# Grid attention with the values as weights in both column halves, and the sinks' exponentials for eight steps at once

## The chip, the cores and the metric

One core of one Trainium2 chip runs the whole program. The metric is the device time in microseconds, the median of the runs. All times below are microseconds.

## The reference

A block of two transformer layers is followed by a second block of two. The second block's first mixer, called the grid mixer here, is the part that is changed: grouped-query attention with 16 query heads over 4 groups of keys and values, head width 64, over 256 context tokens and 256 latent tokens, with a learned sink in the softmax.

```python
def softmax_with_sink(s, sink):
    sk = sink.astype(jnp.float32)[None, :, :, None, None]
    m = jnp.maximum(jnp.max(s, axis=-1, keepdims=True), sk)
    e = jnp.exp(s - m)
    return e / (jnp.sum(e, axis=-1, keepdims=True) + jnp.exp(sk - m))

# context tokens attend to the 256 context keys
s_c = jnp.einsum('bqhgd,bkhd->bhgqk', q_ctx, k_ctx)
o_ctx = jnp.einsum('bhgqk,bkhd->bqhgd', softmax_with_sink(s_c, sink_g), v_ctx)
# latent tokens attend to latent keys at most 128 away and to all context keys
p = softmax_with_sink(jnp.concatenate([s_lat, s_ctx], axis=-1), sink_g)
o_lat = einsum(p[..., :n_loc], v) + einsum(p[..., n_loc:], v_ctx)
return o_lat @ w_o, o_ctx @ w_o
```

## The kernel before, in words

Each engine has its own program, written out in order, and the engines meet through counting semaphores (`up` raises one, `wait_ge` waits for a named point of it). An engine runs its list strictly in order, so an instruction that waits holds everything behind it. Large products are made of three passes of fp32r (high times high, high times low, low times high); the attention itself is in plain fp32, where TensorE makes two passes of each matmul. A weight chunk comes by DMA into `raw`, ScalarE (ACT) rounds it into `WH` (line 439), VectorE (DVE) makes the rest `WL` (line 452), two chunks ahead of use (`act_begin`, `dve_begin`).

The grid mixer (`grid_pe`, `grid_act`, `grid_dve`, `grid_pool`) first projects keys, values and the queries of group 0. Then comes a loop of 34 **slots**. Slot n = 8g + p works on pair p of group g. A pair is two heads on the same 128 query tokens; the two heads' queries stand in the two halves of the partitions. Pairs 0 to 3 of a group (`seg` 0) are the context tokens with 256 keys (n=256), pairs 4 to 7 the latent tokens with 512 keys (n=512). In the text a slot is named by its p. In slot n TensorE does, in this order:

1. `scores` of pair n into PSUM banks 4 and 5, which must have been read by DVE;
2. one step of `queries(g+1)`, while g < 3: in p0 to p3 a quarter of the projection of the next group's queries (24 passes), in p7 eight transposes of those queries, nothing in p4 to p6;
3. `pv` (probabilities times values) of pair n-2 and `turn_p` (transposes of the probabilities) of pair n-1, each head by head: pv even, turn even, pv odd, turn odd.

In `pv` the turned probabilities `cPT` (128 keys x 128 queries) are the weights and 64 columns of the values are moved, so the output has the queries on the partitions: 2 matmuls a head for n=256, 4 for n=512, each two passes. All 8 steps of a `seg` go into bank 7.

DVE adds the mask and takes the maximum (line 2455), copies the sink behind the scores (2456), and makes the negated maximum (2458), once for each head; then it copies the odd head's turned probabilities (2467). ACT takes the exponential with its sum (2401), so the sink is the 257th or 513th element; it copies the even head's turned probabilities (2410) between the two exponentials, and evacuates the projected queries in p4 (2383, 2385) and their transposes in p7 (2393). After 8 steps DVE takes the reciprocal of the sums (2474) and multiplies bank 7 into `cO` (2478), which frees the bank. In p0 of groups 1 and 2, ACT rounds a weight chunk behind its two exponentials, and DVE makes the low part ahead of the odd head's copy.

After slot 33 `turn_o_pe` turns the whole output (32 transposes) and ACT and DVE split it into `XH` and `XL` (1113, 1120); then the output products (`last_products_pe`) begin. They go through features 0 to 511 of all four output blocks before they come to feature 512, and two of the weight chunks are made long before.

Of the kernel before, what the change touches and what calls it, by code (L numbers as in the profile page):

```python
# [8 lines left out]
F32 = mybir.dt.float32  # L9
# [6 lines left out]
KT = 8  # L16
# [133 lines left out]
class Program:  # L150
# [106 lines left out]
    def phase_views(self):  # L257
# [30 lines left out]
        self.cSM = [v(H, 5120 + 520 * i, [128, 520]) for i in range(2)]  # L288
        self.cSM += [v(H, 11280, [128, 520]), v(self.tmp_at, 3072, [128, 520])]
        self.cPT = [v(H, 6160 + 512 * i, [128, 512]) for i in range(2)]  # L290
        self.cO = v(H, 7184, [128, 4096]).rearrange("p (b d) -> p b d", b=4)
# [823 lines left out]
    def turn_o_dve(self, tag, h):  # L1115
        dve = self.dve
        for k2 in range(4):
# [3 lines left out]
            self.xl.name((tag, 2 * k2 + 1))  # L1121

# [1104 lines left out]
    def grid_pe(self):  # L2227
# [87 lines left out]
        def pv(g, i):  # L2315
            seg, hd, o = self.GRID_STEPS[i]
            n = 4 if seg else 2
            pe.wait_ge(self.emptied if i % 2 else self.evac, ("grid", "p", g, i))
# [5 lines left out]
            m.then_inc(*self.weighed.up(("grid", g, i)))  # L2324
            if i % 8 == 7:
                self.empties([7], (self.o_done, ("grid", g, seg)))
# [4 lines left out]
        for n in range(34):  # L2331
# [6 lines left out]
            for j in range(2):  # L2338
                if n > 1:
                    g, p = divmod(n - 2, 8)  # L2340
                    pv(g, 2 * p + j)
                if 1 <= n < 33:
                    g, p = divmod(n - 1, 8)
                    turn_p(g, 2 * p + j)
        for h in range(2):
            self.turn_o_pe(f"go{h}", self.cO[:, 2 * h:2 * h + 2, :], (self.o_done, ("grid", 3, 1)), h)
        self.rest_grid = self.last_products_pe("grid", w_o, self.x_both(("go0", "go1")), None, True)

    def grid_act(self):
# [4 lines left out]
        nm, dens = self.small[:, 108:112], [self.small[:, 160 + 8 * i:168 + 8 * i] for i in range(2)]  # L2354
# [40 lines left out]
        def score(g, i):  # L2395
            seg, hd, o = self.GRID_STEPS[i]
            u, n = i % 4, 512 if seg else 256
            act.wait_ge(self.v_step, ("grid", "neg", g, i))
            if g:
                act.wait_ge(self.v_step, ("grid", "recip", g - 1, seg))  # L2400
            act.e.activation(self.cSM[u][:, 0:n + 1], self.cSM[u][:, 0:n + 1], ACT.Exp, bias=nm[:, u:u + 1], scale=0.125, accum_out=dens[seg][:, 4 * o + hd:4 * o + hd + 1]).then_inc(*self.expd.up(("grid", g, i)))
# [9 lines left out]

        for _ in queries(0):
# [14 lines left out]
        for h in range(2):  # L2427
            self.turn_o_act(f"go{h}", h)
        self.last_products_act("grid", True, 0, 0, [(self.turned, ("go1", "o", 3))])

    def grid_dve(self):
        dve, PS = self.dve, self.PS
        sk8 = self.small[:, 88:104]
        mx, nm = self.small[:, 104:108], self.small[:, 108:112]
# [10 lines left out]
        def score(g, i):  # L2445
            seg, hd, o = self.GRID_STEPS[i]
            b, u, n = 4 + i % 2, i % 4, 512 if seg else 256
            SM = self.cSM[u]
            col = sk8[:, 4 * g + hd:4 * g + hd + 1]
            dve.wait_ge(self.scored, ("grid", g, i))  # L2450
            dve.wait_ge(self.ld_masks, "grid")
            dve.wait_ge(self.v_step, ("grid", "sink"))
            if (g, i) > (0, 3):
                dve.wait_ge(self.turned, ("grid", "p", g, i - 4) if i > 3 else ("grid", "p", g - 1, i + 12))
# [14 lines left out]
        def pv(g, i):  # L2469
            if i % 8 < 7:  # L2470
                return
# [552 lines left out]
```

## Time and profile before

| | us |
|---|---|
| median of 3 runs (lowest, highest) | 2503.65 (2498.86, 2504.4) |
| the profiled execution: its own time | 2499.47 |
| the profiled execution: its span | 2498.2 |
| busy in the span: TensorE matmuls | 2326.4 (93%) |
| busy: VectorE | 1221.8 (49%) |
| busy: ScalarE | 969.2 (39%) |
| busy: GpSimd | 506.6 (20%) |
| mean granted TensorE clock | 0.961 |
| grid mixer's loop, first scores to last `pv` | from 1437.2 to 1580.2 |
| first output product | 1586.91 |

Busy time is a share of the whole span, over stages with different limits. The granted clock is a share of 2.4 GHz; its two levels are 1 and 0.5. In the tables of instructions PE is TensorE's matmuls and PEld its weight loads, and both carry the line of a helper: 466 for matmuls, 475 for transposes.

### The profile page before, as it was taken

The numbers are of one execution on the slowest core, as the hardware profiler recorded it, in microseconds if no ns is written. First come the engines' busy times: TensorE is split into PE (matmuls) and PEld (weight loads), VectorE is DVE, ScalarE is ACT, GpSimd is POOL, SyncE is SP. The second block draws the span as 40 slices with busy tenths as digits, with TensorE's granted clock in tenths as the row PEclk, the third lists the DMA queues.
The fourth block names the chain that finished last, engine by engine and source line by source line (L and its number), as shares of the span: only waits on it lengthen the run. The fifth ranks groups of instructions, "written<-read, shape, count | busy, mean of one in ns | idle before, by whom it ended". The sixth has DMA issues, their size and how long they took to land.

```text
span 2498.2 us, 37765 instructions
## 1 busy us (share of the span) xinstructions
PE 2326.4 (93%) x16663; PEld 2120.0 (85%) x16663; DVE 1221.8 (49%) x1521; ACT 969.2 (39%) x1145; POOL 506.6 (20%) x453
## 2 busy tenths in 40 slices
PE   6999999989999999889999899979999989888998
PEld 6998899979999998557999877867888877657997
DVE  5645566646555543445655345362122264545444
ACT  3433344434343433334444244333222233534442
POOL 2112434302111211220221101012202210230220
PEclk9999999989999999789999999989999999999999
DMA  6555433445555555666554310113332322213551
GB/s 242 175 173 173 139 122 133 136 169 174 182 179 185 180 182 173 229 237 236 172 183 155 124 35 18 34 68 101 101 98 88 102 96 85 68 51 93 181 183 68
DMA packets 205245, 344.72 MB, mean 138 GB/s; under 512 B 8845, under 2 KB 69498, under 8 KB 205082
## 3 DMA queue, kind: packets, MB, share of 16 engines
q1 hardware_dynamic: 205082, 342.31, 41.0%
q8 instruction: 131, 2.15, 0.3%
q14 instruction: 32, 0.26, 0.0%
HBM read 341.24 MB, written 1.05 MB: 137 GB/s over the span
## 4 chain that ended last, share of the span: by engine, by line
PE 80%; DVE 9%; POOL 4%; ACT 4%; issue 2%; SPq 0%; DMA 0%; DVEq 0%; POOLq 0%; ACTq 0%
PE PS L466 77%; PE PS L475 3%; DVE WL L452 2%; ACT WH L439 1%; POOL small L1454 1%; DVE rstd L587 1%; DVE XL L634 1%; POOL TMP L1463 1%; DVE XL L1002 0%; DVE al L998 0%; POOL small L1452 0%; DVE TMP L1382 0%; POOL TMP L1464 0%; DVE TMP L1387 0%; DVE al L1371 0%
## 5 line engine op out<-in xcount | busy, mean ns | idle before, releaser
L452 DVE TENSOR_TENSOR WL<-raw,WH 128x2048 fp32r<-128x2048 f32 (+2 forms) x281 | 651.6, 2331 | 720.7 <-ACT WH L439 720.7
L466 PE MATMUL PS<-XH,WH 128*128 128x256 f32 (+1 forms) x2336 | 699.3, 299 | 40.3 <-issue 15.3
L466 PE MATMUL PS<-XL,WH 128*128 128x256 f32 (+1 forms) x2336 | 692.9, 297 | 0.0
L466 PE MATMUL PS<-XH,WL 128*128 128x256 f32 (+1 forms) x2336 | 692.6, 297 | 0.0
L439 ACT ACTIVATE WH<-raw 128x2048 fp32r<-128x2048 f32 (+2 forms) x281 | 518.8, 1858 | 361.6 <-PE PS L466 361.1
L466 PEld LDWEIGHTS PS<-XH,WH 128*128 128x128 f32 x2336 | 451.6, 193 | 56.6 <-issue 18.5
L466 PEld LDWEIGHTS PS<-XL,WH 128*128 128x128 f32 x2336 | 452.6, 194 | 10.1
L466 PEld LDWEIGHTS PS<-XH,WL 128*128 128x128 f32 x2336 | 452.2, 194 | 10.0
L466 PE MATMUL PS<-WH,XH 128*128 128x256 f32 (+2 forms) x944 | 287.3, 304 | 17.3 <-DVE XL L634 8.5
L466 PE MATMUL PS<-WL,XH 128*128 128x256 f32 (+2 forms) x944 | 279.1, 296 | 0.0
L466 PE MATMUL PS<-WH,XL 128*128 128x256 f32 (+2 forms) x944 | 278.9, 295 | 0.0
L466 PE MATMUL PS<-HH,WH 128*128 128x256 f32 x960 | 273.5, 285 | 3.4 <-DVE WL L452 3.4
L466 PE MATMUL PS<-HL,WH 128*128 128x256 f32 x960 | 272.9, 284 | 0.0
L466 PE MATMUL PS<-HH,WL 128*128 128x256 f32 x960 | 272.8, 284 | 0.0
L466 PE MATMUL PS<-al,al 128*128 128x64 f32 (+8 forms) x1376 | 224.5, 342 | 16.5 <-DVE al L2882 6.0
L466 PEld LDWEIGHTS PS<-al,al 128*128 128x128 f32 (+4 forms) x1376 | 164.3, 196 | 64.5 <-issue 37.1
L466 PEld LDWEIGHTS PS<-WH,XH 128*128 128x128 f32 x944 | 186.0, 197 | 35.3 <-issue 22.2
L466 PEld LDWEIGHTS PS<-HH,WH 128*128 128x128 f32 x960 | 185.6, 193 | 3.6 <-DVE WL L452 3.6
L466 PEld LDWEIGHTS PS<-WL,XH 128*128 128x128 f32 x944 | 186.4, 197 | 2.5
L466 PEld LDWEIGHTS PS<-WH,XL 128*128 128x128 f32 x944 | 186.2, 197 | 2.5
L466 PEld LDWEIGHTS PS<-HL,WH 128*128 128x128 f32 x960 | 185.6, 193 | 0.1
L466 PEld LDWEIGHTS PS<-HH,WL 128*128 128x128 f32 x960 | 185.5, 193 | 0.0
(232 smaller groups left out, 2573.2 us busy)
## 6 DMA issues: line engine op xcount, KB each, us to landing
raw<-in_ffn_w_in SPq DMA_DIRECT2D x88, 1024.0 KB, 5.1
raw<-in_w_mod SPq DMA_DIRECT2D x48, 1024.0 KB, 5.2
raw<-in_ffn_w_out SPq DMA_DIRECT2D x40, 1024.0 KB, 4.9
raw<-in_a_w_in SPq DMA_DIRECT2D x36, 1024.0 KB, 4.9
raw<-in_w_mlp_in SPq DMA_DIRECT2D x32, 1024.0 KB, 5.5
raw<-in_w_mlp_out SPq DMA_DIRECT2D x32, 1024.0 KB, 5.0
raw<-in_gla_w_in SPq DMA_DIRECT2D x12, 1024.0 KB, 5.0
raw<-in_attn_w_qkv SPq DMA_DIRECT2D x6, 1024.0 KB, 5.0
```

Source lines behind the costliest of these rows:

```text
L439: act.e.activation(self.WH[q % NW][:, 0:nk * nn], self.raw[j % NRAW][:, 0:nk * nn], ACT.Copy).then_inc(*self.hi.up(j))
L452: dve.e.tensor_tensor(self.WL[j % NRAW][:, 0:nk * nn], self.raw[j % NRAW][:, 0:nk * nn], wh.bitcast(F32), ALU.subtract).then_inc(*self.lo. ...
L466: return self.pe.e.matmul(out, l, r, start=start, stop=stop, skip_group_check=skip)
L475: return self.pe.e.transpose(out, i, self.ident if n == 128 else self.CST[0:n, IDENT:IDENT + n])
L587: dve.e.reciprocal(rs, rs).then_inc(*self.rstd_.up(tag))
L634: dve.e.scalar_tensor_tensor(self.XL[slot][:, k, :], R[:, k, :], self.COL[:, at + k:at + k + 1], self.XH[slot][:, k, :].bitcast(F32), ALU. ...
L1454: pool.e.tensor_tensor(rs, rs, self.MH[:, 0:8], ALU.pow).then_inc(*self.p_step.up(key("pow")))
L1463: pool.e.tensor_tensor(q[:, :, :, 0:32], x[:, :, :, 32:64], bc(0, 32), ALU.mult)
```

## The change

In `pv` the operands change places. 64 columns of the values are the weights, and the turned probabilities of 128 queries are moved. The even head's output goes to partitions 0 to 63, the odd head's to 64 to 127, that is to the two column halves of the array, with the two heads' matmuls alternating. The output has its features on the partitions, as the output products need it. So the 32 transposes at the end go away, and the division can no longer be by a number per partition. The reciprocals, one per query and head, are spread by ACT to 64 columns each (`cRD`, 128x512) and turned by TensorE (`sums`, 4 transposes per group and `seg`), ACT copies bank 7 to `cO`, DVE multiplies `cO` by the turned reciprocals, and ACT and DVE split the result into `XH` and `XL`, partly in slots 27 to 33. The two heads' `pv` stand together, ahead of both `turn_p`. The sink is no longer a column of the scores: one negation serves two heads, and per 8 steps DVE makes an argument of 8 columns, ACT its exponential, and DVE adds it to the sums.

```diff
+        def pv(g, i0):
+            seg, hd, o = self.GRID_STEPS[i0]
+            pair, n = hd // 2, 4 if seg else 2
+            pe.wait_ge(self.evac, ("grid", "p", g, i0))
+            pe.wait_ge(self.emptied, ("grid", "p", g, i0 + 1))
             pe.wait_ge(self.evac, ("grid", "in", 5, 1))
-            if i % 8 == 0:
+            if i0 % 8 == 0:
                 self.pe_bank(7)
             for k in range(n):
-                m = self.mm(PS[:, 7, o * 256 + hd * 64:o * 256 + hd * 64 + 64], self.cPT[i % 2][:, k * 128:k * 128 + 128], self.cV[:, k, g * 64:g * 64 + 64], k == 0, k == n - 1)
+                for j in range(2):
+                    m = self.mm(PS[64 * j:64 * j + 64, 7, pair * 256 + o * 128:pair * 256 + o * 128 + 128], self.cV[:, k, g * 64:g * 64 + 64], self.cPT[j][:, k * 128:k * 128 + 128], k == 0, k == n - 1, True)
...
+            if i0 % 8 == 6:
+                self.empties([7], (self.evac, ("grid", "o", g, seg)))
+                sums(g, seg)
+        def sums(g, seg):
+            nonlocal spare
+            b = spare = self.GRID_SPARE[spare]
+            pe.wait_ge(self.evac, ("grid", "r", g, seg))
+            self.pe_bank(b)
+            for pair in range(2):
+                for o in range(2):
+                    m = self.tr(PS[:, b, pair * 256 + o * 128:pair * 256 + o * 128 + 128], self.cRD[:, 256 * o + 128 * pair:256 * o + 128 * pair + 128])
...
-            for j in range(2):
-                if n > 1:
-                    g, p = divmod(n - 2, 8)
-                    pv(g, 2 * p + j)
-                if 1 <= n < 33:
-                    g, p = divmod(n - 1, 8)
+            if n > 1:
+                g, p = divmod(n - 2, 8)
+                pv(g, 2 * p)
+            if 1 <= n < 33:
+                g, p = divmod(n - 1, 8)
+                for j in range(2):
                     turn_p(g, 2 * p + j)
-        for h in range(2):
-            self.turn_o_pe(f"go{h}", self.cO[:, 2 * h:2 * h + 2, :], (self.o_done, ("grid", 3, 1)), h)
```

On ACT:

```diff
+            if i % 8 == 7:
+                act.wait_ge(self.v_step, ("grid", "sinks", g, seg))
+                act.e.activation(e8, e8, ACT.Exp).then_inc(*self.expd.up(("grid", "sinks", g, seg)))
+        def recips(g, seg):
+            act.wait_ge(self.v_step, ("grid", "recip", g, seg))
+            if g or seg:
+                act.wait_ge(self.turned, ("grid", "r", g, 0) if seg else ("grid", "r", g - 1, 1))
+            act.e.activation(self.cRD.rearrange("p (h d) -> p h d", d=64), rd.unsqueeze(2).to_broadcast([128, 8, 64]), ACT.Copy).then_inc(*self.evac.up(("grid", "r", g, seg)))
+        def out(g, seg):
+            act.wait_ge(self.weighed, ("grid", g, 8 * seg + 7))
+            act.e.activation(self.cO[:, seg, 2 * g:2 * g + 2, :], PS[:, 7, :].rearrange("p (k t) -> p k t", k=2), ACT.Copy).then_inc(*self.evac.up(("grid", "o", g, seg)))
         for n in range(34):
             g, p = divmod(n, 8)
+            if n > 4 and n % 4 == 1:
+                recips(*divmod(n // 4 - 1, 2))
...
+            if n > 4 and n % 4 == 1:
+                out(*divmod(n // 4 - 1, 2))
+            if 27 <= n < 33:
+                seg, g3 = divmod(n - 27, 3)
+                split(g3, seg)
+            if n == 33:
+                split(3, 0)
+        split(3, 1)
...
```

On DVE:

```diff
+        def score(g, i0):
+            for i in (i0, i0 + 1):
...
+                dve.e.tensor_tensor_reduce(self.cSM[u][:, 0:n], PS[:, b, 0:n], self.CST[:, 512 * o:512 * o + n], 1.0, sk8[:, 4 * g + hd:4 * g + hd + 1], ALU.add, ALU.max, mx[seg][:, c:c + 1]).then_inc(*self.maxed.up(("grid", g, i)))
+            dve.wait_ge(self.maxed, ("grid", g, i0 + 1))
+            dve.e.tensor_scalar(nm[seg][:, c - 1:c + 1], mx[seg][:, c - 1:c + 1], -0.125, None, ALU.mult).then_inc(*self.v_step.up(("grid", "neg", g, i0)))
...
+        def out(g, seg):
+            O = self.cO[:, seg, 2 * g:2 * g + 2, :]
+            dve.wait_ge(self.evac, ("grid", "o", g, seg))
+            dve.wait_ge(self.turned, ("grid", "r", g, seg))
+            dve.e.tensor_tensor(O, O, PS[:, self.bank_of["grid", "r", g, seg], :].rearrange("p (k t) -> p k t", k=2), ALU.mult).then_inc(*self.o_done.up(("grid", g, seg)))
         for n in range(34):
             g, p = divmod(n, 8)
+            if n and n % 4 == 0:
+                recips(*divmod(n // 4 - 1, 2))
+            if n > 4 and n % 4 == 2:
+                out(*divmod((n - 2) // 4 - 1, 2))
             if n < 32:
                 score(g, 2 * p)
-                score(g, 2 * p + 1)
```

On DVE, `recips(g, seg)` waits for the exponential of the sinks, adds it to the sums and takes the reciprocal; it stands ahead of the scores of p4 and p0. On ACT the spreading stands ahead of the exponentials of p5 and p1, and the copy of bank 7 behind them.

## Rows read from the trace of the kernel before

**Rows 1.** The page: chain that ended last, share of the span by engine.

```profile
PE 80%; DVE 9%; POOL 4%; ACT 4%; issue 2%; SPq 0%; DMA 0%; DVEq 0%; POOLq 0%; ACTq 0%
```

**Rows 2.** Busy time by stretch: start:end length, engines busy (instructions), granted clock, DMA.

```profile
1508.00:1546.00 38.00, 35.80 (x277) 29.80 (x277) 19.80 (x79) 17.47 (x45) 4.62 (x8) 1.00 0.09 29
...
1581.20:1584.60 3.40, 3.36 (x16) 3.36 (x17) 1.39 (x2) 1.69 (x3) 0.00 (x0) 0.50 0.00 0
```

**Rows 3.** Groups by form, 1438 to 1582: busy, mean ns of one | idle before.

```profile
L466 PE MATMUL PS<-al,al 128*128 128x64 f32 x384 | 51.7, 271 | 3.7 <-DVE al L2478 3.7
...
L2455 DVE CUSTOM_DVE_ANT_0 al<-PS,CST,small 128x512 f32<-128x512 f32 x32 | 23.8, 745 | 6.9 <-PE PS L466 6.9
```

**Rows 4.** Timeline of weight loads in the later GLA mixer: start, length, what.

```profile
2169.66 0.64 PEld L466 LDWEIGHTS PS<-al,al 128*64 128x64 f32 x8 [0.33 <-issue]
2170.68 0.73 PEld L466 LDWEIGHTS PS<-al,al 128*128 128x128 f32 x4 [0.39 <-issue]
2171.74 0.64 PEld L466 LDWEIGHTS PS<-al,al 128*64 128x64 f32 x8 [0.33 <-issue]
```

**Rows 5.** Timeline of weight loads, p4 to p7 of group 1 (64*128: scores).

```profile
1495.13 0.30 PEld L466 LDWEIGHTS PS<-al,al 64*128 64x128 f32 x4 [0.17 <-issue]
1496.19 0.52 PEld L466 LDWEIGHTS PS<-al,al 128*128 128x128 f32 x4 [0.76 <-issue]
...
1498.02 0.33 PEld L466 LDWEIGHTS PS<-al,al 64*128 64x128 f32 x4 [0.57 <-DVE small L2455]
...
1500.98 0.30 PEld L466 LDWEIGHTS PS<-al,al 64*128 64x128 f32 x4 [0.17 <-DVE small L2455]
...
1505.56 0.30 PEld L466 LDWEIGHTS PS<-al,al 64*128 64x128 f32 x4 [0.17 <-issue]
...
1510.93 0.42 PEld L475 LDWEIGHTS PS<-CST,al 128*128 128x128 f32 x4 [1.23 <-ACT al L2401]
1511.52 0.30 PEld L466 LDWEIGHTS PS<-al,al 64*128 64x128 f32 x4 [0.17 <-issue]
```

**Rows 6.** Timeline of DVE and ACT in the same p4.

```profile
1496.30 0.75 DVE L2455 CUSTOM_DVE_ANT_0 al<-PS,CST,small 128x512 f32<-128x512 f32 x1 [0.63 <-PE PS L466]
...
1497.28 0.72 ACT L2401 ACTIVATE al<-al,small 128x513 f32<-128x513 f32 x1 [1.78 <-DVE small L2458]
...
1498.00 0.36 ACT L2410 ACTIVATE al<-PS 128x256 f32<-128x256 f32 x1
1498.26 0.71 ACT L2401 ACTIVATE al<-al,small 128x513 f32<-128x513 f32 x1
...
1498.97 0.58 ACT L2383 ACTIVATE TMP<-PS 128x512 f32<-128x512 f32 x1
1499.44 0.59 ACT L2385 ACTIVATE TMP<-PS 128x512 f32<-128x512 f32 x1
```

**Rows 7.** Timeline of all engines, p0 (from 1473.1) and p1 (from 1479.3) of group 1.

```profile
1478.13 0.60 ACT L2410 ACTIVATE al<-PS 128x512 f32<-128x512 f32 x1 [3.02 <-PE PS L475]
...
1479.12 1.90 ACT L439 ACTIVATE WH<-raw 128x2048 fp32r<-128x2048 f32 x1
...
1481.05 2.29 DVE L452 TENSOR_TENSOR WL<-raw,WH 128x2048 fp32r<-128x2048 f32 x1 [6.00 <-ACT WH L439]
...
1483.26 0.68 DVE L2467 COPY al<-PS 128x512 f32<-128x512 f32 x1
```

**Rows 8.** Chain that ended last, 1430 to 1620: start, length, what.

```profile
1503.90 0.44 PE PS L475 x4
1504.35 0.84 PE PS L466 x8
...
1578.27 1.90 PE PS L466 x16
...
1580.19 0.22 DVE small L2474
...
1586.91 33.20 PE PS L466 x186
```

More of the change, by code:

```diff
@@ L1121, in turn_o_dve, with split_o_act, split_o_dve @@
             self.xl.name((tag, 2 * k2 + 1))
+    def split_o_act(self, tag, g, h, O, ready):
+        for signal, key in ready:
+            self.act.wait_ge(signal, key)
+        self.act.e.activation(self.XH[h][:, 2 * g:2 * g + 2, :], O, ACT.Copy).then_inc(*self.xh.up((tag, 2 * g)))
+    def split_o_dve(self, tag, g, h, O):
+        self.dve.wait_ge(self.xh, (tag, 2 * g))
+        self.dve.e.tensor_tensor(self.XL[h][:, 2 * g:2 * g + 2, :], O, self.XH[h][:, 2 * g:2 * g + 2, :].bitcast(F32), ALU.subtract).then_inc(*self.xl.up((tag, 2 * g)))
+        self.xl.name((tag, 2 * g + 1))
     def attn_out_pe(self, tag, O, ready, w_out):
@@ L2353, in grid_act @@
         KD = TMP[:, 1024:3072].rearrange("p (b g u d) -> p b g u d", b=4, g=4, u=2)
-        nm, dens = self.small[:, 108:112], [self.small[:, 160 + 8 * i:168 + 8 * i] for i in range(2)]
+        nm, dens = [self.small[:, 32 + 8 * i:40 + 8 * i] for i in range(2)], [self.small[:, 160 + 8 * i:168 + 8 * i] for i in range(2)]
+        e8, rd = self.small[:, 48:56], self.small[:, 116:124]
         self.act_begin()
@@ L2426, in grid_act @@
                 next(nxt, None)
-        for h in range(2):
-            self.turn_o_act(f"go{h}", h)
-        self.last_products_act("grid", True, 0, 0, [(self.turned, ("go1", "o", 3))])
+            if n > 4 and n % 4 == 1:
[6 more added lines that the diff above has]
+        split(3, 1)
+        self.last_products_act("grid", True, 0, 0, [(self.xl, ("go1", 6)), (self.weighed, ("grid", 3, 15))])
     def grid_dve(self):
@@ L2433, in grid_dve @@
         sk8 = self.small[:, 88:104]
-        mx, nm = self.small[:, 104:108], self.small[:, 108:112]
+        mx, nm = [[self.small[:, at + 8 * i:at + 8 * i + 8] for i in range(2)] for at in (16, 32)]
+        e8 = self.small[:, 48:56]
         dens, rd = [self.small[:, 160 + 8 * i:168 + 8 * i] for i in range(2)], self.small[:, 116:124]
@@ L2492, in grid_dve @@
                 turn_p(g, 2 * p + 1)
-            if n > 1:
-                g, p = divmod(n - 2, 8)
-                pv(g, 2 * p + 1)
-        for h in range(2):
-            self.turn_o_dve(f"go{h}", h)
+            if 28 <= n < 34:
+                seg, g3 = divmod(n - 28, 3)
+                split(g3, seg)
+        out(3, 1)
+        split(3, 0)
+        split(3, 1)
         self.last_products_dve("grid", True, 0, 0, None)
@@ L2534, in gla_sp @@
         wd = self.gWD.rearrange("p (k e r) -> p k e r", e=2, k=KT)
-        sp.wait_ge(self.o_done, ("grid", 3, 1))
+        sp.wait_ge(self.xl, ("go1", 6))
         sp.e.dma_start(self.CST[:, 0:512], A["const"][:, RESET:RESET + 512]).then_inc(*self.ld_masks.up("reset"))
```

71 lines of the change are left out of this document (33 added, 38 removed).

## The prediction

> **What bounds the kernel now.** I read four views. First the page's chain of work that ended last: TensorE carries 80% of it, DVE and ACT 13% together [rows 1]. So a change pays if it takes time from TensorE's own queue, or from a wait of that queue. Second, busy time by stretch: in the loop of slots TensorE is busy 35.8 of 38 us at the full clock [rows 2], so the loop is nearly, but not quite, TensorE's. Third, the groups by form: the old `pv` is 384 passes of 64 columns [rows 3]. Fourth, timelines and the chain, for the waits. p4 takes 2.9 us, p5 3.0, p6 4.6, p7 6.0 [rows 5], 16.4 together, and in each TensorE waits somewhere: in p7 its transposes wait 1.23 for ACT. The whole end, from the last `pv` at 1580.2 to the first output product at 1586.9, is a hand-over in which TensorE only turns [rows 8]. I write S for the start of a slot's scores.
>
> **What TensorE does less.** Eight old passes (one head, n=512) take 0.84 [rows 8], a pair 1.68; with n=256 half of it, 0.84. There are 16 pairs of each: 40.3 us. The trace of before has no probabilities moved past 64-wide weights, but the GLA mixer has plain fp32 passes into column halves: eight of 256 columns take 1.02 (2169.66 to 2170.68), no more than four full-width ones (2170.68 to 2171.74, 1.06) [rows 4]. So the halves run side by side. A new pair with n=512 is 16 passes of 128 columns, the same columns: 1.02. With n=256 it is half, 0.51, plus about 0.1, as the drain at the ends doesn't shrink: 0.6. Bounds: 0.9 and 1.9 for the large pair (the latter if they ran one after another), 0.5 and 1.0 for the small. New total 16 x 1.62 = 25.9, a gain of 14.4. Against it: going over to column halves costs 0.1 where a projection stands before it (12 pairs, 1.2; four transposes of 0.44 plus the switch to the scores are 0.59 in [rows 5]), and `sums` adds 4 transposes, 0.44 [rows 8], seven times in the loop: 3.1. TensorE's own work falls by 10 us.
>
> The Trainium skill (TensorEngine Tiling (Array Packing), Theoretical Speedup) gives up to 2x for a dimension of 64; rows 4 agree, 1.02 against 1.06 for twice the passes. The same page (PSUM Bottleneck) says that tiling doesn't speed up the emptying of PSUM; by the first rule alone the loop would gain the 10 us, by the second nothing, and the walk below shows which holds.
>
> **What the waits do.** I walk the queues with the durations of the rows. On ACT an exponential of 512 takes 0.72, a copy of 256 0.26 and of 512 0.48 until the next may start, the two evacuations 1.06 [rows 6]. DVE's first maximum starts 1.17 after S, and before it is followed by exponential 1 after 0.98 [rows 5, 6]; now both maxima (2 x 0.745 [rows 3]) and one negation come first, so exponential 1 starts 1.7 after the first maximum. New small operations are taken as 0.2, from the reciprocal's 0.22 [rows 8]; the spread copy as 0.6, from 0.59 [rows 6] (bounds 0.2 and 0.8); DVE's multiplication as 0.7, from the copy's 0.68 [rows 7]. `pv` now wants both heads' copies at once, and between the odd turn and that `pv` stand only scores.
>
> *p4.* DVE's first maximum waits 0.3 for the sinks' exponential and the sum. The next scores wait for the maxima: 2.9, as before.
>
> *p5.* Exponential 1 of p4 starts 3.05 after p4's S. ACT's queue then holds 0.72, copy 0.26, 0.72, evacuations 1.06, spread copy 0.6: 3.4. So the spread reciprocals are there at 6.5, that is 3.55 after p5's S. `sums` waits for them from 1.9 on (1.65 us idle), then 0.44, two turns 0.88, switch 0.1: p5 lasts 5.0 instead of 3.0. Behind `sums` the turns wait, and for them ACT and DVE.
>
> *p6.* Bank 7 is free after ACT's exponential, copy, exponential and copy of the bank, 6.5 after p5's S, 1.5 after p6's; before, it waited for DVE's division. 1.5 + 1.02 + 0.88, with the next scores waiting for maxima behind the multiplication: 3.7 instead of 4.6.
>
> *p7.* Exponential 1 at 2.9, 0.72, copy 0.5 (its turn ends about 3.4), 0.72, the sinks 0.2, evacuation 0.6: the second turn's bank is free 5.7 after S, then 0.44 and 0.1: 6.3 instead of 6.0. It idles 2.2 us, as TensorE arrives earlier and ACT later.
>
> Sum of p4 to p7: 17.9 against 16.4. The same walk over the old queues gives 16.2, so its latencies are 0.1 to 0.2 short: +1.6.
>
> *p0 and p1* (groups 1, 2). The old odd copy ends at 1483.94, at the end of a chain: turn, ACT's copy at 1478.13, `WH` at 1479.12, `WL` at 1481.05, copy at 1483.26 [rows 7], 10.9 after p0's S. The chain is bound to the turn, which now comes 0.2 to 0.3 later in p0 (1.02 and a switch instead of 0.84), so nothing on TensorE can shorten it. Before, the even `pv` and a turn ran under it; now the whole pair waits 2.0 us, then 1.02, `sums` 0.44, turns 0.46, switch 0.1. From 11.2: 13.2 against 12.2 (1473.1 to 1485.3): +1.0.
>
> *p2, p3:* 0.6 + 0.1 instead of 0.84: -0.1 each. *Group 3* has no projections: its first four slots gain 0.5, the rest loses 0.9, its last `pv` 0.1 earlier: +0.3. *Group 0* has nothing in flight in p0: p2 to p7 alone, +1.4.
>
> Loop: 2 x (1.6 + 1.0 - 0.2) + 1.4 + 0.3 = +6.5. The 10 us of TensorE's work come back as waits, and more: ACT's queue sets p5 and p7, the weight chunk p1.
>
> **The end.** From 1580.2 (`pv`'s result seen by DVE) to 1586.9 there are 6.7 us, 6.9 from TensorE's last pass [rows 8]. Now `sums` takes 0.44 and the products follow at once: weights of two chunks are made, features 0 to 255 split. The last output (copy, multiplication, two splits, 3 us) is wanted only at feature 768, after more than 10 us of products. -6.4. ACT's and DVE's eight splits are moved, not added: seven lie in slots with a free projection step or at the end. SP's waiting DMA of GLA's constants is hidden by the MLP that follows.
>
> Sum at full clock: +6.5 - 6.4 = +0.1. The walk came out short on the old queues, never long, so I take +0.5.
>
> **The clock.** Before, the loop ran at 1.00, and the only fall was after TensorE idled in the end part: 3.4 us at 0.50 [rows 2], inside the 6.9 already counted. New are ten idles of 1.6 to 2.3 us (p5 four times, p7 three, p1 two, one in group 3), longer than that before the fall (about 1.1). A fall of 3.4 us at half rate costs up to 1.7. I take two falls: +2.5 to 3.4. The Trainium skill (TensorE: Matmul & The Clock Gate, What's actually happening) has the clock fall after an idle window and rise after a busy one; the fall at 1581.2 agrees, and it says nothing of how partial idles in this loop count.
>
> Forecast: +0.5 + 2.5 = +3. The sum is made in one profiled execution of 2498.2 span and 2499.47 own time, 4.2 under the median of the runs, 2503.65; a difference carries over: **2506.7**. Its own range is 2501 to 2511.
>
> **Rivals.**
> *The waits don't grow (faster).* If ACT's queue in p5 and p7 is shorter than walked (spread copy 0.2, exponentials back to back), only the end counts and perhaps part of the 10 us: -6 to -16, 2488 to 2498. For: 35.8 of 38 us busy [rows 2]. Against: old waits are there already, and each new one has its queue in the rows. It decides if the loop's growth stays under 1.4, that is under 0.35 a group. Chance 0.15.
> *The clock falls at most of the ten idles.* 6 to 10 falls of 1.7: +10 to +17, 2514 to 2521. For: shorter idles have done it. Against: the old waits of p6 and p7 (0.8, 1.2) never did. Chance 0.25.
> *The halves run one after another.* 16 x (0.85 + 0.4) less what waits swallow: +16, 2520. Against: rows 4. Chance 0.04.
> *Forecast:* 0.56.
>
> **Chances and range.** What a measurement of this kernel can tell from no change is about 0.2%, 5 us: 2498.6 to 2508.7. Faster 0.15, from the first rival. Same 0.45, four fifths of the forecast's case. Slower 0.40: the two other rivals, 0.29, and the forecast's upper fifth, 0.11. The range that leaves out most of the first rival and the top of the others is 2498 to 2518.
>
> **What would show it.** In the profile after: 64-wide loads with eight starts in about 0.9 us (else the third rival); in p5 four transposes that wait some 1.6 us for ACT's spread copy, in p7 a turn that waits 2.2 for ACT's evacuation, in p1 a `pv` that waits 2.0 for DVE's copy behind `WL`; p4 to p7 near 18 us; the loop 6 to 8 us longer at full clock and the first product within 1 us of the last `pv`; stretches at 0.50 between 1437 and 1590 counted. The prediction is wrong if the loop is not longer, or if the clock falls often.

## The result: 0.17% slower, and the profile after

| | before | changed |
|---|---|---|
| median, us (runs) | 2498.86 (20) | 2504.94 (20) |
| lowest to highest | 2495.84 to 2504.52 | 2502.82 to 2506.79 |
| profiled execution: own time, span | 2499.47, 2498.2 | 2504.21, 2502.9 |
| first scores to first output product | 1437.19 to 1586.91, 149.7 | 1437.62 to 1590.76, 153.1 |
| granted clock, mean | 0.961 | 0.958 |

The ratio is 1.0017, 95% interval [1.0011, 1.0023]: slower by 0.17%, about 4 us. That is a real difference, and it lies within the 0.2% that the prediction named as "the same". The 2503.65 of the small table above was the median of three runs that lay high. Against the 20 runs the medians are 6.1 apart, against the ratio 4.2.

The chain that ended last has the shape of [rows 1], with TensorE's share a little lower:

```profile
PE 78%; DVE 9%; ACT 5%; POOL 4%; issue 3%; SPq 0%; DMA 0%; DVEq 0%; POOLq 0%; ACTq 0%
```

In the code of the changed kernel TensorE's helper lines stand one further: 467 for matmuls, 476 for transposes. Busy time by stretch (columns as in [rows 2]) shows what happened to TensorE in the loop:

```profile
1470.00:1508.00 38.00, 32.00 (x244) 24.70 (x240) 14.47 (x45) 17.07 (x44) 2.37 (x5) 0.91 0.09 29
1508.00:1546.00 38.00, 33.16 (x268) 25.30 (x264) 17.09 (x52) 16.10 (x44) 2.24 (x4) 0.96 0.09 29
...
1517.80:1521.20 3.40, 3.40 (x17) 2.75 (x15) 1.78 (x8) 0.60 (x2) 0.00 (x0) 0.52 0.02 5
```

It was busy 35.8 of 38 us in [rows 2] at the full clock. Now it is busy 33.2 and 32.0, the granted clock is 0.96 and 0.91, and inside these stretches stand pieces of 3.4 us at half clock. DVE is less busy too (17.1 against 19.8). No engine became fuller; all of them wait more.

The two profiles don't start the loop alike, and [rows 2] doesn't show that: in the kernel before the clock is at half until 4.0 us after the first scores, in the changed kernel until 1.6 after them.

```profile
1437.19:1441.20 4.01, 4.01 (x18) 3.36 (x18) 1.27 (x8) 3.88 (x7) 0.00 (x0) 0.50 0.00 0
```

```profile
1437.60:1439.20 1.60, 1.60 (x7) 0.93 (x7) 0.32 (x1) 1.45 (x2) 0.00 (x0) 0.51 0.00 0
```

Group 0's p0, the same work in both, takes 5.47 in the first and 4.39 in the second. The 1.1 us between them are in every comparison of these two loops, and they don't come from the change: a second profile of the kernel before (below) has 4.39 there with the same code. Of the profiles below, five begin like the changed kernel: the low part behind the copy, the spread copy twice, the kernel before with two orders, the first of the sinks' kernel and the second of the kernel before. All others begin like the first profile of before.

The groups by form, first scores to first product:

```profile
L476 PE MATMUL PS<-CST,al 128*128 128x128 f32 x220 | 32.6, 287 | 11.9 <-ACT al L2423 6.2 <-ACT al L2448 5.7
...
L467 PE MATMUL PS<-al,al 128*64 128x128 f32 x381 | 28.3, 283 | 9.5 <-DVE al L2524 5.7 <-ACT al L2455 2.6 <-ACT al L2442 0.6
```

The new `pv` is 28.3 us of busy time where the old one was 51.7 [rows 3]. Behind the bar stand the new idles: 11.9 us ahead of transposes, for ACT's evacuation of the turned queries (2423) and for ACT's spread reciprocals (2448), and 9.5 ahead of `pv`, mostly for DVE's copy (2524).

The weight loads of p4 to p7 of group 1, to be laid beside [rows 5]. Scores are the `64*128` rows and start the slots; `128*64` is the new `pv`:

```profile
1499.81 0.30 PEld L467 LDWEIGHTS PS<-al,al 64*128 64x128 f32 x4 [0.17 <-issue]
1500.86 0.42 PEld L467 LDWEIGHTS PS<-al,al 128*64 128x64 f32 x8 [0.76 <-ACT al L2442]
1501.45 0.42 PEld L476 LDWEIGHTS PS<-CST,al 128*128 128x128 f32 x4 [0.17 <-issue]
1502.51 0.33 PEld L467 LDWEIGHTS PS<-al,al 64*128 64x128 f32 x4 [0.64 <-DVE small L2508]
1503.77 0.42 PEld L467 LDWEIGHTS PS<-al,al 128*64 128x64 f32 x8 [0.93 <-ACT al L2442]
1505.96 1.29 PEld L476 LDWEIGHTS PS<-CST,al 128*128 128x128 f32 x12 [1.77 <-ACT al L2448]
1507.42 0.30 PEld L467 LDWEIGHTS PS<-al,al 64*128 64x128 f32 x4 [0.17 <-issue]
1508.99 0.88 PEld L467 LDWEIGHTS PS<-al,al 128*64 128x64 f32 x16 [1.27 <-ACT al L2455]
1510.04 0.86 PEld L476 LDWEIGHTS PS<-CST,al 128*128 128x128 f32 x8 [0.17 <-issue]
1511.07 0.32 PEld L467 LDWEIGHTS PS<-al,al 64*128 64x128 f32 x4 [0.17 <-DVE small L2508]
...
1516.88 0.42 PEld L476 LDWEIGHTS PS<-CST,al 128*128 128x128 f32 x4 [2.27 <-ACT small L2433]
1517.47 0.34 PEld L467 LDWEIGHTS PS<-al,al 64*128 64x128 f32 x4 [0.17 <-issue]
```

A large pair takes 1.05 (1508.99 to 1510.04), a small one 0.59 (1500.86 to 1501.45). p5 starts at 1502.51; its twelve transposes (four of `sums`, eight turns) are held for 1.77 by the spread copy and p5 lasts 4.9. p7 starts at 1511.07 and its second turn is held for 2.27. Here the label names ACT's small exponential (2433), but that one had been done for 0.6 us; what is missing is the evacuation right behind it on ACT (2423), as the same wait on the matmul side says (2.06 there).

ACT in the same p4 and p5, to be laid beside [rows 6]:

```profile
1502.64 0.72 ACT L2430 ACTIVATE al<-al,small 128x512 f32<-128x512 f32 x1 [1.97 <-DVE small L2510]
...
1503.36 0.36 ACT L2442 ACTIVATE al<-PS 128x256 f32<-128x256 f32 x1
1503.62 0.71 ACT L2430 ACTIVATE al<-al,small 128x512 f32<-128x512 f32 x1
...
1504.33 0.58 ACT L2413 ACTIVATE TMP<-PS 128x512 f32<-128x512 f32 x1
1504.80 0.59 ACT L2415 ACTIVATE TMP<-PS 128x512 f32<-128x512 f32 x1
1505.28 0.63 ACT L2448 ACTIVATE al<-small 128x512 f32<-128x512 f32 x1
```

From 1502.64 to 1505.9 ACT has not a gap, and the spread copy stands last. It reads only eight numbers per partition, and the reciprocal that makes them had ended at 1501.1, 4.2 us before.

p1 of group 1 (its scores start at 1480.8), to be laid beside [rows 7]:

```profile
1481.49 1.90 ACT L440 ACTIVATE WH<-raw 128x2048 fp32r<-128x2048 f32 x1
...
1483.43 2.29 DVE L453 TENSOR_TENSOR WL<-raw,WH 128x2048 fp32r<-128x2048 f32 x1 [7.27 <-ACT WH L440]
1485.63 0.68 DVE L2524 COPY al<-PS 128x512 f32<-128x512 f32 x1
...
1486.46 1.54 PE L467 MATMUL PS<-al,al 128*64 128x128 f32 x16 [1.87 <-DVE al L2524]
```

TensorE had turned the odd head's probabilities by 1480.9. They lay in PSUM for 4.7 us, until DVE's copy at 1485.63: 2.5 us of that are the last part of DVE's idle of 7.27, for its next instruction was `WL`, which waited for ACT, and 2.2 are `WL` itself. The pair then took 1.48 (1486.46 to 1487.94) instead of 1.03, as the clock fell 0.5 us after it had begun.

And the end, the chain that ended last:

```profile
1589.32 1.09 PE PS L467 x16
1591.00 29.04 PE PS L467 x155
```

The last `pv` ends at 1590.4. Behind it stand only the four transposes of `sums`, and the first product's matmul begins at 1590.76, 0.4 us later (this chain counts it from the end of the transposes, 1591.00). In the kernel before the same distance was 6.7, from 1580.2.

### The profile page after: what moved, and what is told of

It is laid out like the page before. It is cut to its first block, busy times and chain, and to the rows that moved or that the text cites. A ratio compares the mean times of both kernels' runs of the same rounds, so it can differ in the third digit from the quotient of the medians.

```text
span 2502.9 us, 37728 instructions
## 1 busy us (share of the span) xinstructions
PE 2315.0 (92%) x16663; PEld 2102.0 (84%) x16663; DVE 1216.8 (49%) x1433; ACT 976.9 (39%) x1169; POOL 506.7 (20%) x453
## 3 DMA queue, kind: packets, MB, share of 16 engines
HBM read 341.24 MB, written 1.05 MB: 137 GB/s over the span
## 4 chain that ended last, share of the span: by engine, by line
PE 78%; DVE 9%; ACT 5%; POOL 4%; issue 3%; SPq 0%; DMA 0%; DVEq 0%; POOLq 0%; ACTq 0%
PE PS L467 75%; PE PS L476 3%; DVE WL L453 2%; ACT WH L440 1%; POOL small L1467 1%; DVE rstd L588 1%; DVE XL L635 1%; POOL TMP L1476 1%; ACT al L2430 0%; DVE XL L1003 0%; DVE al L999 0%; POOL small L1465 0%; ACT al L2442 0%; DVE TMP L1395 0%; POOL TMP L1477 0%
## 5 line engine op out<-in xcount | busy, mean ns | idle before, releaser
L467 PE MATMUL PS<-al,al 128*128 128x64 f32 (+9 forms) x1376 | 199.9, 344 | 23.0 <-DVE al L2948 6.1
L467 PEld LDWEIGHTS PS<-al,al 128*128 128x128 f32 (+4 forms) x1376 | 135.6, 180 | 74.0 <-issue 30.6
```

The source lines that it names most:

```text
L467: return self.pe.e.matmul(out, l, r, start=start, stop=stop, skip_group_check=skip)
```

## The experiments

All times below are medians. "Mixer" is first scores to first output product in the profile of that kernel. It compares code better than a span, for this reason: from the first product on, all kernels here run the same code, and yet that part took 909.3 to 917.6 us from profile to profile, with 70 to 91 us of it at half clock. The clock makes differences inside the mixer too: 1.1 us by its start, as said above, and 1.1 to 1.6 for each fall. The order of the list is that of the argument; each of the first four undoes one order that the change had brought or left in place.

**Negation for each head.** In `score` on DVE the negation goes back into the loop over the two heads.

```diff
-            dve.wait_ge(self.maxed, ("grid", g, i0 + 1))
-            dve.e.tensor_scalar(nm[seg][:, c - 1:c + 1], mx[seg][:, c - 1:c + 1], -0.125, ...)
+                dve.wait_ge(self.maxed, ("grid", g, i))
+                dve.e.tensor_scalar(nm[seg][:, c:c + 1], mx[seg][:, c:c + 1], -0.125, ...)
```

> The changed kernel, but DVE negates each head's maximum right behind it, as before the change, instead of one negation for both. Theory of the queues: ACT's first exponential of a pair starts 0.7 us earlier, which shortens p5's wait for the spread copy by 0.8 in each of four groups, but DVE's second maximum ends 0.13 later in the slots that wait for it; together 2 to 3 us faster than the changed kernel. Rival, the clock: the ten new waits matter only through falls of the clock; the long waits of p7 and p1 stay, so nothing changes (within 1 us).

Measured: 2502.98 (11 runs), ratio to before 1.0016 [1.0005, 1.0027]; mixer 151.6, against 153.1 of the changed kernel. p4 to p7 17.2 instead of 17.7: p5 4.01 (4.88), p6 3.85 (3.66), p7 6.38 as before. Exponential 1 starts earlier, so p5's spread copy does; in p7 it changes nothing, as ACT waits there for the turn, not for the negation. It gives about 2 us, as the theory of the queues had it (1.6 by the mixers, 2.6 when the slower start of this profile is taken off).

**The turned reciprocals one slot later.** On TensorE `sums` moves from behind `pv` of the last pair to behind the turns of the slot.

```diff
-                sums(g, seg)
...
                 for j in range(2):
                     turn_p(g, 2 * p + j)
+            if n > 4 and n % 4 == 1:
+                sums(*divmod(n // 4 - 1, 2))
```

> The changed kernel, but TensorE turns the spread reciprocals behind the turns of the probabilities of the same slot instead of ahead of them. Theory of the queues: p5's wait of 1.65 us becomes one of 0.8, four times, and part of it comes back at bank 7 in p6: 2 to 3 us faster than the changed kernel. Rival: what the turns are spared, the multiplication by the turned reciprocals loses; no change within 1 us.

Measured: 2500.39 (11), 1.0008 [0.9999, 1.0017]; mixer 151.3. p5 4.00, p6 3.95, p4 to p7 17.1. The wait itself fell from 1.77 to 0.75:

```profile
1502.39 0.85 PEld L476 LDWEIGHTS PS<-CST,al 128*128 128x128 f32 x8 [0.17 <-issue]
1504.00 0.42 PEld L476 LDWEIGHTS PS<-CST,al 128*128 128x128 f32 x4 [0.75 <-ACT al L2449]
...
1506.43 0.88 PEld L467 LDWEIGHTS PS<-al,al 128*64 128x64 f32 x16 [1.55 <-ACT al L2456]
```

A part comes back in p6, where `pv` waits 1.55 for the copy of bank 7 (1.27 in the changed kernel): ACT is the same distance behind, TensorE only arrives earlier. The mixer is 1.8 shorter, 2.9 with the start taken off: the theory's 2 to 3.

**The low part of the weight chunk behind the odd head's copy.** On DVE, `WL` and the copy change places in p0.

```diff
-                if g < 3 and p == 0:
-                    self.dve_begin()
             if 1 <= n < 33:
                 g, p = divmod(n - 1, 8)
                 turn_p(g, 2 * p + 1)
+            if n < 24 and n % 8 == 0:
+                self.dve_begin()
```

> The changed kernel, but in p0 DVE makes the low part of the weight chunk behind the odd head's copy instead of ahead of it. Theory of the queues: the 2.0 us wait of the value products in p1 goes, twice, less what the later low part costs (nothing, it is made two chunks ahead), and one of the three falls of the clock with it: 3.5 to 5 us faster than the changed kernel. Rival: the wait is TensorE's arrival and moves to the next slot's maxima or to the low part's user, then 0 to 1 us.

Measured: 2500.35 (11), 1.0004 [0.9995, 1.0012]; mixer 149.4, 3.8 less (forecast 3.5 to 5). p1 5.84 in both groups, where it was 9.00 (with a fall of the clock) and 7.68. DVE in the same place:

```profile
1480.05 0.69 DVE L2524 COPY al<-PS 128x512 f32<-128x512 f32 x1 [4.78 <-PE PS L476]
1482.54 2.29 DVE L453 TENSOR_TENSOR WL<-raw,WH 128x2048 fp32r<-128x2048 f32 x1 [1.79 <-ACT WH L440]
```

Nothing waits for `WL` in this place: the price of its turn in the queue was paid by `pv` alone. The fall of the clock after p1 is gone, those after p7 stay, and one more appears in group 3.

**The turned queries ahead of the exponentials.** On ACT the evacuation of the turned queries goes ahead of p7's exponentials.

```diff
+                if p == 7:
+                    next(nxt, None)
                 score(g, 2 * p)
...
                 score(g, 2 * p + 1)
-                next(nxt, None)
+                if p < 7:
+                    next(nxt, None)
```

> The changed kernel, but in p7 ACT evacuates the next queries' transposes ahead of its first exponential instead of behind the second one and the sinks' exponential. Theory of the queues: ACT is idle there until the maxima are made, so the two copies fit in, the 2.25 us wait of the second turn in p7 goes, three times, and with it two of the three falls of the clock: 6 to 9 us faster than the changed kernel. Rival: bank or exponential then holds the turn as long (the exponential starts 0.3 later), at most 2 us.

Measured: 2498.32 (11), 0.9997 [0.9988, 1.0006]; mixer 144.5, 8.7 less. p7 is 4.13 in every group, where it was 6.38. That is 6.8 us for three groups. This profile has one fall of the clock where that of the changed kernel has three, which is worth 3.0 us, and it starts 1.1 slower. One exchange of order on ACT takes back the whole loss.

**The spread copy made twice.** The suspected wait in p5, made larger: ACT spreads the reciprocals, waits for itself and spreads them again.

```diff
+            act.e.activation(self.cRD..., rd..., ACT.Copy).then_inc(*self.a_step.up(("grid", "first", g, seg)))
+            act.wait_ge(self.a_step, ("grid", "first", g, seg))
             act.e.activation(self.cRD..., rd..., ACT.Copy).then_inc(*self.evac.up(("grid", "r", g, seg)))
```

> The changed kernel, with ACT's spread copy of the reciprocals made twice, each behind a signal of the one before: ACT's queue is 0.6 to 0.7 us longer in eight slots. Theory of the queues: ACT sets p5 in four groups, and there the whole length comes through; in p1 it has room. 2.5 to 3 us slower than the changed kernel. Rival, TensorE bound or clock bound: no change within 1 us, and if every slot pays, 5 us.

Measured: 2507.45 (5), 1.0040 [1.0028, 1.0053], 2.5 above the changed kernel's median; mixer 157.6, 4.4 more. The second copy costs ACT 0.66:

```profile
1505.65 0.63 ACT L2448 ACTIVATE al<-small 128x512 f32<-128x512 f32 x1
1506.31 0.63 ACT L2450 ACTIVATE al<-small 128x512 f32<-128x512 f32 x1
1506.85 0.71 ACT L2430 ACTIVATE al<-al,small 128x512 f32<-128x512 f32 x1
```

and TensorE's idle there grows from 1.53 by the same 0.66:

```profile
1507.00 2.29 PE L476 MATMUL PS<-CST,al 128*128 128x128 f32 x12 [2.19 <-ACT al L2450]
```

So p5 hangs on the spread copy one for one; group 3, without a fall, shows it in the length of the slot too (5.10, was 4.43). In groups 0 to 2 p5 grew by more, to 6.56, 6.29 and 6.06 (4.88 before): the clock fell in each of them, where it had not fallen after an idle of 1.53. The two p1 waits brought a fall each, and the three of p7, as long as in the changed kernel (2.06), now brought none. The falls in the mixer went from three to five. So of the 4.4 us some 2.6 are the queue and the rest is the clock.

**The two heads of `pv` one after another.** All matmuls of the even head, then all of the odd head, instead of alternating. The work is the same.

```diff
-            for k in range(n):
-                for j in range(2):
+            for j in range(2):
+                for k in range(n):
```

> The changed kernel, but the value products of the even head are issued all before those of the odd head, instead of alternating. Theory: TensorE takes weight loads and passes of the other column half ahead of those that wait, as in the GLA mixer, where two matmuls of one half precede two of the other and still run side by side; with 8 passes a head they still do: same time within 1 us. Rival: the halves run side by side only where they alternate, then 16 large pairs cost up to 0.85 and 16 small 0.4 more: 8 to 16 us slower.

Measured: 2513.45 (5), 1.0053 [1.0041, 1.0066]; mixer 161.4, 8.3 more, with three falls as in the changed kernel. The same pair in this kernel:

```profile
1510.47 1.55 PE L467 MATMUL PS<-al,al 128*64 128x128 f32 x16 [0.47 <-ACT al L2455]
1511.95 1.09 PE L476 MATMUL PS<-CST,al 128*128 128x128 f32 x8
```

It takes 1.48 (1510.47 to 1511.95) instead of 1.03. In the trace, taken matmul by matmul, each half starts one every 0.109 us, and in the changed kernel the two halves start within 0.04 us of each other all along. Here the odd head's first starts at 1510.93, 0.46 after the even head's first and ahead of the even head's last three (1511.03 to 1511.25). So the halves still run side by side, but only over the last part of the first head. Were nothing side by side it would be 16 x 0.109 = 1.74. The small pairs lose nothing: four matmul passes of one head ahead of four of the other take 0.60 (0.59 in the changed kernel), with the two halves starting 0.01 apart. The theory holds for them and fails for eight passes a head, and the rival is right about the large pairs only: 16 x 0.45 = 7.2 of the 8.3, the other 1.1 being the loop's start. p6 and p7 grow by this 0.45 each (4.10, 6.87). p1 grows by 0.7 to 9.75 in group 1 and by 2.1 to the same 9.75 in group 2, where the changed kernel had its fall in p0 and this one has it in p1.

**The kernel before with two of the orders.** Low part behind the copy, turned queries ahead of the exponentials, nothing else.

> The kernel before with two of the changes of order, the low part behind the odd copy and the queries' transposes evacuated first. It tells how much of the gain of the reordered changed kernel is due to the order alone. Theory of the queues: of before's waits the 1.2 us of p7 go, three times, and up to 0.3 in p1, but the even and odd products already covered the rest: 3 to 4 us faster than the kernel before. Rival: the orders alone are worth as much there as in the changed kernel, 10 us.

Measured: 2498.58 (11), 0.9996 [0.9987, 1.0005]; mixer 143.4, 6.4 less than before. p7 4.65 (5.96), p1 5.82 (5.95). These make 4.2, as the theory had it; the other 2.2 are the clock at the loop's start and a fall in the old end part, neither of which is in the second profile of before (below, 147.5). The mixer is clearly shorter, and the runs hardly are: behind the mixer this profile took 915.2 us, with 84.2 at half clock, where that of the kernel before took 911.3 with 70.5. Whether the shorter mixer caused that or the two profiles merely differ, these runs don't settle; the second profile of before (below) has 914.3 there with unchanged code.

**The changed kernel with all four orders.** The four edits above together (each head's negation, `sums` later, `WL` later, queries first).

> The changed kernel with four changes of order only: each maximum negated at once, the turns of the reciprocals behind the turns of the probabilities, the low part behind the odd copy, the queries' transposes evacuated first. The work of every engine is the same but for 32 negations. Theory of the queues: with the waits gone the 10 us of TensorE's work show: 14 us faster than the changed kernel at full clock and 4 more as no fall is left, that is 15 to 19, and 9 to 13 faster than the kernel before. Rival, TensorE's passes: the exchanged operands save little, the changed kernel is bound by TensorE; then at most the falls, 4 us.

Measured: 2485.76 (5 runs, 2482.76 to 2488.56), 0.9948 [0.9935, 0.9961]: faster than both kernels, by 13 and by 19 us. Mixer 134.3, no fall of the clock in it once it is at full clock 4.0 us after its start, p4 to p7 14.3. Its loop by stretch and its weight loads of p4 to p7 of group 1 (p4 starts at 1489.72, 2.9 ahead of the first row):

```profile
1470.00:1508.00 38.00, 36.28 (x310) 28.17 (x310) 20.90 (x71) 20.33 (x53) 4.62 (x8) 1.00 0.09 29
```

```profile
1492.62 0.33 PEld L467 LDWEIGHTS PS<-al,al 64*128 64x128 f32 x4 [0.83 <-DVE small L2512]
1493.70 0.42 PEld L467 LDWEIGHTS PS<-al,al 128*64 128x64 f32 x8 [0.76 <-ACT al L2443]
1494.29 1.32 PEld L476 LDWEIGHTS PS<-CST,al 128*128 128x128 f32 x12 [0.17 <-issue]
1495.78 0.30 PEld L467 LDWEIGHTS PS<-al,al 64*128 64x128 f32 x4 [0.17 <-issue]
1497.63 0.88 PEld L467 LDWEIGHTS PS<-al,al 128*64 128x64 f32 x16 [1.55 <-ACT al L2456]
...
1499.88 0.33 PEld L467 LDWEIGHTS PS<-al,al 64*128 64x128 f32 x4 [0.34 <-DVE small L2512]
```

The idle of 1.77 ahead of the twelve transposes is gone and p5 is 3.2 (1492.62 to 1495.78). What is left is p6's wait for the copy of bank 7.

**Three of the four orders** (the pair's one negation stays).

> The changed kernel with three of the four new orders: turned reciprocals one slot later, low part of the weight chunk behind the odd head's copy, evacuation of the turned queries ahead of the exponentials of p7; the one negation for a pair stays. If the gains of the orders add up (each alone: 1.9, 4.6, 6.6 us of first scores to first product, the negation 1.6), first scores to first product is 140 us, about 6 more than with the fourth, and the total about 2491. Rival: with the other three waits gone, the pair's negation is no longer covered or no longer matters: 134 to 136, total 2486 as with all four.

Measured: 2491.02 (6 runs, 2489.23 to 2492.36), 0.9957 [0.9944, 0.9971]; mixer 136.6, p4 to p7 14.8. Neither number of the expectation was hit: the mixer lies between the two, nearer to the rival's. So the negation is worth 2.2 us of mixer beside the others, about what it was worth alone (1.6, or 2.6 at the same start). The gains alone on which the expectation rested weren't of one kind: 1.9 was a difference of mixers, 4.6 and 6.6 were differences of medians. By the mixers they are 1.8, 3.8 and 8.7, and three orders together would give 139.

**The sinks' part alone, on the kernel before.** On DVE `score`, the argument of 8 columns and the addition to the sums as in the changed kernel, on ACT the small exponential; operands, division and turning as in the kernel before.

```diff
+            dve.wait_ge(self.expd, ("grid", "sinks", g, seg))
+            dve.e.tensor_tensor(dens[seg], dens[seg], e8, ALU.add).then_inc(*self.v_step.up(("grid", "sum", g, seg)))
+            dve.wait_ge(self.v_step, ("grid", "sum", g, seg))
             dve.e.reciprocal(rd, dens[seg])...
```

> The kernel before with one part of the change alone: one negation for the two heads of a pair, no column for the sink, and per 8 steps the argument on VectorE, its exponential on ScalarE and the addition to the sums; operands, division and turning of the output as before. Theory: the small operations saved on VectorE lie beside other work, and the pair's one negation lets exponential 1 start about 0.7 later, so p7, which waits for ScalarE's evacuation in the kernel before (5.96 us), grows to 6.3 to 6.6; first scores to first product 149.7 us in the kernel before, here 151 to 153, total +1 to +3. Rival: the queue of VectorE is shorter by 128 copies and 64 negations, and that shortens the waits for the maxima in p4 to p6: first scores to first product 147 to 149, total -1 to -3.

Measured: 2511.29 (12), 1.0038 [1.0026, 1.0049]. That is far more than either expectation. Yet the mixer of its profile is 151.3, only 1.6 above the first profile of before and 3.8 above the second, which starts alike (1.6 of that is a fall in group 3's p0), and p4 to p7 16.7 (2.74, 3.09, 4.78, 6.11) against 16.4. The profile belonged to the lowest run, 2500.27; the other eleven are 2510.0 to 2513.0. So it was profiled again.

> The kernel with the sinks' part alone, profiled a second time: its profile came out at 2500.27 us, its other eleven runs at 2510 to 2513, with a mean granted clock 0.002 to 0.006 lower. Theory: the code's own length is the same (first scores to first product 151 us and slots as in the first profile), and the 10 us are time at half clock outside the grid mixer, in code that is the same in all kernels here. Rival: in those runs the clock falls several times inside the grid mixer, at the idle of p7, and first scores to first product is 156 to 161 us.

Measured: 2512.06, mixer 163.3, with every slot of groups 0 and 1 the same to 0.01 but for one (group 0's first, 5.47 against 4.39). The theory fell and the rival named the right place with the wrong shape. Two falls are of the usual length, one in group 2's p0 (1.5 us more) and one in the end part (1.2 more), and the loop starts 1.1 slower. The rest is one long fall in group 3. By stretch:

```profile
1552.60:1564.50 11.90, 11.34 (x52) 9.34 (x52) 4.54 (x19) 3.16 (x10) 0.00 (x0) 0.50 0.00 0
1564.50:1576.50 12.00, 12.00 (x46) 7.68 (x45) 4.23 (x15) 4.71 (x16) 0.00 (x0) 0.50 0.00 1
```

TensorE ran at the lower level for 23.9 us on end, although it was busy for 23.3 of them. Group 3 took 32.1 from its first scores to the scores of its last pair, against 22.0 for its slots in profiles without a fall: 10 us lost. It began 1.9 us after the wait of p7 in group 2:

```profile
1550.71 0.63 PE L475 MATMUL PS<-CST,al 128*128 128x128 f32 x4 [1.28 <-ACT al L2394]
```

In the first profile the same wait, 1.27 long, stands at the same place, and the fall behind it lasted 3.4. I can't say from these runs why one lasted seven times as long as the other. Nor is it shown that the other eleven runs above, 2510 to 2513, had this long fall; there is no profile of them. Their mean granted clock, 0.953 to 0.957, is below that of the first profile (0.959), as that of the second (0.953) is.

**The kernel before, profiled again.**

> The kernel before, profiled a second time, to see how far two profiles of one program differ. Its runs lie in two heaps, about 2497 to 2499 and 2503 to 2504, the second with a mean granted clock 0.004 to 0.005 lower. Expected: the grid mixer's slots as in the first profile to 0.05 us, first scores to first product 149.7 with 1.7 more for each further fall of the clock in it, and the other differences in stretches of half clock outside the grid mixer. Rival: slots differ by more than 0.1 us at the same clock.

Measured: 2500.95, mixer 147.5. Slots agree to 0.01 but for group 0's first (4.39, was 5.47). There is no fall of the clock in this mixer; in the first profile there is one, in the end part [rows 2]. The first slot and the end part, 1.1 us each, make the 2.2 us between the mixers, so all of it is the clock. So one profile of this program stands within some 2 us in the mixer and 3 us behind it.

## Why the prediction was right

**TensorE's own work.** Forecast 25.9 for all pairs. The rows give 1.03 to 1.05 and 0.59, so 16 x 1.04 + 16 x 0.59 = 26. That the halves run side by side held, for large pairs in full only with the heads' matmuls alternating.

**The queues.** The walk stood up slot by slot. p4 2.9 forecast, 2.73 measured; p5 5.0 and 4.88; p6 3.7 and 3.67; p7 6.3 and 6.38; p4 to p7 17.9 and 17.66. The growth is 1.3 instead of 1.6, as the correction for the walk's shortness on the old queues wasn't needed. p0 and p1: 13.2 forecast; measured without the clock's falls 5.74 (p0 of the kernels in which it didn't fall there) and 7.68, 13.4. The three waits were where they were looked for, 1.77 in p5, 2.27 in p7 and 1.87 in p1 (forecast 1.65, 2.2, 2.0), and each has an experiment that takes its cause away or doubles it.

**The end.** -6.4 forecast. The first product comes 0.4 after the last `pv` instead of 6.7: -6.4 (counted to the matmul's start). As the prediction says, the old end had a fall of the clock in it; the second profile of before, without one, has 1.1 us less there.

**The loop.** From first scores to last `pv` it grew from 143.0 to 152.8, by 9.8. The three falls of the clock make 4.6 of it: 0.2 in p7 of group 0, p0 7.03 and 7.25 instead of 5.74, p1 9.01 instead of 7.68, p2 5.10 instead of 4.87. Against them stands the 1.1 us that the old loop lost at its start. The prediction says that the old loop ran at 1.00; for its first 4.0 us it ran at 0.50, and this term is missing from its sum. With both taken out the loop grew by 6.3 at the full clock, against 6.5 forecast, and by groups 1.2 (forecast 1.4), 2.4 and 2.3 (2.4 each) and 0.4 (0.3). Loop and end together are about -0.1, where the walk had +0.1 and the forecast took +0.5.

**The clock, mis-sized.** Forecast: two falls, +2.5. It fell three times, after p7 of groups 0 and 1 and in p1 of group 1, and cost 4.6, some 1.5 each. Less the 1.1 of the old loop's start the clock is +3.5. The rival had 6 to 10. Of the ten idles nine are there (p5 four times, the last only 1.1 long, p7 three, p1 two); the longest other one in group 3 is 0.9. The falls don't follow the length of an idle alone. On the matmul side, in the profiles named: 1.53 in p5 never brought one and 2.19, with the doubled copy, did three times of three; but 2.06 in p7 did twice of three in the changed kernel and never in the one with the doubled copy. In the old kernel 1.13 in p7 never had one in two profiles, 1.09 in its end part had one in the first and none in the second, and the sinks' kernel fell at 1.27 and 1.28. What else decides it is not shown. The Trainium skill (TensorE: Matmul & The Clock Gate, What's actually happening) says of this that an idle window lets the clock fall and a busy one raises it. Each fall in the mixers above came behind an idle, but a short one between matmuls, so these rows neither confirm nor refute the first half. The 23.9 us at half clock with TensorE busy for 23.3 of them are not what the second half gives.

**The sum.** +3.0 was forecast. The mixers of the two profiles differ by 3.4, the spans by 4.7, the ratio says 4.2. The errors of two terms were opposite: -0.6 at full clock and +1.0 for the clock. So the mechanism was right and its two parts nearly so. How the 4.2 divides is less sure, for each kernel has one or two profiles. Against the second profile of before, which has no fall and the changed kernel's start, the mixer grew by 5.6: 4.6 are falls of the clock, and only 1.0 is work and waits. So in these profiles the new waits cost more through the clock than by their length. That the absolute time came out so close, 2506.7 for 2504.94, is luck: the base of 2503.65 was 4.8 above what 20 runs gave, and the medians moved by 6.1 where +3 was forecast.

**Where the saved time went.** With all four orders the change is worth 9.0 us of mixer against the kernel before with its two (134.3, 143.4), 10.1 if both loops started alike, and 12.8 in the medians. Of the 10.1, 5.5 come from the end (last slot to product 8.48 against 13.99). Of TensorE's 10 us only some 4.6 reach the clock on the wall even then. So the saving is in the kernel, and the orders of ACT and DVE in p0, p5 and p7 had covered it. The first rival, "the waits don't grow", becomes true once they are changed.

## What to carry to other kernels

A change that takes work off the busiest engine must be followed by a look at the order of the other engines' queues: here instructions that were not urgent (a weight chunk's low part on DVE, two exponentials on ACT, TensorE's turns of the reciprocals) stood ahead of one that TensorE needed or could have done at once, and a negation waited for a second maximum. Four changes of order gave 19 us, while the change itself gave a loss. An idle of TensorE can cost more than its length, since behind it the clock may fall: with 6.8 us of idle taken out, the mixer was 8.7 shorter. Compare stretches of code, not spans, look up the granted clock at both ends of a stretch before comparing it, and don't trust one profile for a few us: the same program gave 2500 and 2512, with one long stretch at half clock between them.

## What the runs showed of the hardware

- Two column halves run side by side, and the order of issue decides over how much: 16 passes of 128 columns took 1.03 us alternating and 1.48 with eight of each half in a row, where the second half started 0.46 late, beside the last three passes of the first. With four of each half in a row nothing was lost (0.60 and 0.59).
- A fall of the clock inside the mixer is mostly 3.4 us long and cost 1.1 to 1.6 us here, but one lasted 23.9 us with TensorE busy 23.3 of them, and cost 10.
- The part behind the mixer is the same code everywhere and took 909 to 918 us, with 70 to 91 us at half clock: roughly, the longer it took, the more of it was at half clock. So some 8 us of a span are the clock's and not the kernel's. What decides them is not shown.
